# Last DeltaNet head and its block inverse: VectorE's panel residuals, tile sums and inverse levels in another order

## What is computed

```
proj = h @ w_in
qkv = silu(causal_depthwise_conv(proj[..., :DN_CONV_DIM], conv_w))
lower = where(strict, einsum("bhncd,bhnkd->bhnck", k_beta, k) * decay, 0)
sol = triangular_solve(lower + eye(CHUNK), rhs, lower=True)
u, w = sol[..., :DN_DV], sol[..., DN_DV:]
def step(state, xs):
    v_new = u_n - w_n @ state
    o = q_n @ state + a_n @ v_new
    state = state * exp(gl_n) + k_n.T @ v_new
o = rmsnorm(o, norm_w) * silu(z)
h = h + o @ w_out
hn = rmsnorm(h, norm_mlp[0]);  h = h + square(relu(hn @ mlp_w_up[0])) @ mlp_w_down[0]
```

## Time and profile before

| | |
|---|---|
| median of 3 runs | 1400.56 us (1398.73 to 1401.97) |
| profiled execution | 1400.85 us |
| its span | 1399.1 us |
| TensorE busy | 1358.9 us, 97% |
| VectorE busy | 793.7 us, 57% |
| ScalarE busy | 532.4 us, 38% |
| GpSimd busy | 250.5 us, 18% |
| mean granted clock of TensorE | 0.993 of full speed |

### The profile page before, as it was taken

The page is one execution under the profiler, slowest core; times in us unless marked ns, Lnnn a source line. Parts: engine busy times, 40 slices in busy tenths (PEclk is TensorE's granted clock), DMA queues, the critical chain, the costliest instruction groups (busy, mean ns, idle before and its releaser), DMA issues.

```text
span 1399.1 us, 18107 instructions
## 1 busy us (share of the span) xinstructions
PE 1358.9 (97%) x6594; PEld 1118.9 (80%) x6594; DVE 793.7 (57%) x1205; ACT 532.4 (38%) x901; POOL 250.5 (18%) x243
## 2 busy tenths in 40 slices
PE   7989999999899999999999999989999999999998
PEld 5778888888778888888888878668888888888877
DVE  5567787777674343343465876764433434335755
ACT  6545545443253141331334421654322323223344
POOL 3545555553031000000012110002010000000211
PEclk9999999999999999999999999999999999999998
DMA  6233332322232223222322353312232322332211
GB/s 177 66 86 86 79 79 62 85 70 71 90 106 91 90 98 113 90 90 93 104 76 89 103 123 70 82 43 94 91 101 94 107 90 90 100 104 98 89 62 60
DMA packets 168575, 125.67 MB, mean 90 GB/s; under 512 B 35873, under 2 KB 165186, under 8 KB 168514
## 3 DMA queue, kind: packets, MB, share of 16 engines
q1 hardware_dynamic: 167410, 123.01, 29.6%
q10 hardware_dynamic: 1104, 1.84, 0.5%
HBM read 116.96 MB, written 5.25 MB: 87 GB/s over the span
## 4 chain that ended last, share of the span: by engine, by line
PE 79%; DVE 11%; ACT 3%; issue 2%; DVEq 2%; DMA 1%; POOL 1%; POOLq 0%; SPq 0%; ACTq 0%
PE psum L148 22%; PE psum L150 22%; PE psum L149 22%; PE psum L898 2%; DVE wL L140 1%; PE psum L909 1%; ACT wH L132 1%; DVE bL L1408 1%; DVEq L1177 1%; DVE hT L1609 1%; DVE terms L1175 1%; DVE acc L1607 1%; PE psum L1928 1%; PE psum L912 1%; PE psum L1935 1%
## 5 line engine op out<-in xcount | busy, mean ns | idle before, releaser
L148 PE MATMUL psum<-aH,wH 128*128 128x512 f32 x896 | 360.4, 402 | 4.0 <-ACT taps L744 3.4
L150 PE MATMUL psum<-aL,wH 128*128 128x512 f32 x896 | 350.7, 391 | 0.0
L149 PE MATMUL psum<-aH,wL 128*128 128x512 f32 x896 | 349.8, 390 | 0.0
L140 DVE TENSOR_TENSOR wL<-wRaw,wH 128x2048 fp32r<-128x2048 f32 (+2 forms) x125 | 240.0, 1924 | 132.7 <-ACT wH L132 127.1
L148 PE MATMUL psum<-bH,wH 128*128 128x512 f32 x720 | 284.6, 395 | 2.3 <-DVE pleT L2054 1.6
L150 PE MATMUL psum<-bL,wH 128*128 128x512 f32 x720 | 280.9, 390 | 0.0
L132 ACT CAST wH<-wRaw 128x2048 fp32r<-128x2048 f32 (+2 forms) x109 | 197.2, 1814 | 219.9 <-PE psum L150 219.9
L149 PE MATMUL psum<-bH,wL 128*128 128x512 f32 x720 | 280.7, 390 | 0.0
L148 PEld LDWEIGHTS psum<-aH,wH 128*128 128x128 f32 x896 | 169.0, 189 | 37.6 <-ACT taps L744 3.9
L150 PEld LDWEIGHTS psum<-aL,wH 128*128 128x128 f32 x896 | 168.5, 188 | 36.1
L149 PEld LDWEIGHTS psum<-aH,wL 128*128 128x128 f32 x896 | 169.1, 189 | 32.0 <-issue 0.5
(11 more groups left out here) (295 smaller groups left out, 1503.4 us busy)
## 6 DMA issues: line engine op xcount, KB each, us to landing
wRaw<-in_mlp_w_up SPq DMA_DIRECT2D x64, 512.0 KB
wRaw<-in_mlp_w_down SPq DMA_DIRECT2D x64, 512.0 KB
wRaw<-in_dn_w_in SPq DMA_DIRECT2D x32, 512.0 KB
wRaw<-in_ple_w_gate SPq DMA_DIRECT2D x16, 512.0 KB
xScaled<-inv_blocks SPq DMA_DIRECT2D x16, 256.0 KB, 3.1
wRaw<-in_sw_w_in SPq DMA_DIRECT2D x16, 256.0 KB
wRaw<-in_sw_w_out SPq DMA_DIRECT2D x16, 256.0 KB
wRaw<-in_dn_w_out SPq DMA_DIRECT2D x8, 384.0 KB
```

Of the source, the lines that this page charges most:

```text
L140: last = [nc.vector.tensor_tensor(o, r, h_.bitcast(F32), ALU.subtract) for o, r, h_ in zip(*([v if half is None else v[:, half * v.shape[1 ...
L148: nc.tensor.matmul(o, wh, xh, start=first, stop=False)
L149: nc.tensor.matmul(o, wl, xh, start=False, stop=False)
L150: return nc.tensor.matmul(o, wh, xl, start=False, stop=last)
```

## The change

It moves instructions of VectorE, and one of ScalarE. In every step but the last: the second half of the residual of the panel in slot 1 goes from before `advance(1)` to behind `residual(2)`; `blocks_inverse(4)` goes before `residual(2)`; `blocks_inverse(8)` is split into its two halves with `solved(2)` between them. At the end of head 7's step the tile sum `out_early_dve(4)` and the next panel's residual go behind the last scan's `advance(0)`. In the last scan the residual of the last output panel comes in halves around `solved(3)` instead of after the scan, `tail(0)` comes before `out_early_dve(6)`, and ScalarE's cast of that panel comes before its `q_part(3)`. In `dn_last_dve` the residual of the MLP's first panel comes in halves behind tiles 1 and 3 instead of ahead of all tiles.

```diff
@@ dn_step_act
             if a is None:
-                for i in range(1, NT):
-                    q_part(i)
+                q_part(1)
+                q_part(2)
                 prep_hi(act, n, n % 2)
+                q_part(3)
                 tail(0)
                 tail(1)
@@ dn_step_dve
             if a is None:
                 solved(0)
                 advance(0)
+                out_early_dve(dve, 4)
+                prep_lo(dve, n - 1, (n - 1) % 2)
                 for i in range(1, NT):
                     residual(i)
+                    if i == 3:
+                        prep_lo(dve, n, n % 2, 0)
                     solved(i)
                     if i == 2:
                         out_early_dve(dve, 5)
+                    if i == 3:
+                        prep_lo(dve, n, n % 2, 1)
                     advance(i)
+                tail(0)
                 out_early_dve(dve, 6)
-                prep_lo(dve, n, n % 2)
-                tail(0)
                 tail(1)
...
-            def blocks_inverse(m):
+            def blocks_inverse(m, parts=(0, 1)):
...
-                for left, right, out_ in ((low, first, hf), (second.rearrange("p q c i -> p q i c"), hf, corner)):
+                steps = ((low, first, hf), (second.rearrange("p q c i -> p q i c"), hf, corner))
+                for left, right, out_ in (steps[i] for i in parts):
...
             residual(1)
             prep_lo(dve, n, 1, 0)
             solved(1)
-            prep_lo(dve, n, 1, 1)
             if p is not None:
                 g_next_dve(dve, p)
             silu_dve(dve, a, 2, a_, reused)
             advance(1)
             pairs_inverse()
             blocks_inverse(2)
+            blocks_inverse(4)
             residual(2)
-            blocks_inverse(4)
+            prep_lo(dve, n, 1, 1)
             if p is None:
                 out_early_dve(dve, 0)
-            solved(2)
             if b is None:
                 silu_dve(dve, p, 0, s, reused)
-            blocks_inverse(8)
+            blocks_inverse(8, (0,))
+            solved(2)
+            blocks_inverse(8, (1,))
             blocks_out()
             advance(2)
...
             grown(2)
-            if p is None:
-                out_early_dve(dve, 4)
-                prep_lo(dve, n + 2, 1)
             dve.drain()
@@ dn_last_dve
-            prep_lo(dve, N_MLP0, N_MLP0 % 2)
             for m in range(KT):
                 dve.wait_ge(tile_done, tiles_before(N_DNLAST) + m + 1)
                 nc.vector.tensor_tensor(hT[:, m, :], bank[2 + m % 4], hT[:, m, :], ALU.add).then_inc(res_ok, 1)
                 if m:
                     next_dve(dve, 0, m - 1)
+                if m in (1, 3):
+                    prep_lo(dve, N_MLP0, N_MLP0 % 2, m // 2)
```

## The result

The changed kernel takes 1404.64 us (median of 12 runs, 1402.43 to 1410.01); the kernel before, run beside it, 1398.46 us (median of 12 runs). The ratio is 1.0044, interval 1.0032 to 1.0056: slower by 0.44%, as forecast in kind, against 0.32% by my sum. The profiled execution of the changed kernel took 1403.45 us with a span of 1401.5 us. I therefore read from the traces where time went, stretch by stretch, and from the medians how much.

A forecast was written before the change was run, and what follows sets the result against it. The prediction took TensorE, busy 1358.9 of 1399.1 us, as the bound, so only its waits and lower-clock stretches count. Its parts, +6.2 + 1.7 - 0.1 - 3.4 = +4.4 us, gave 1405.0 us, range 1397.8 to 1408.0 us.

The forecast's parts named there:

- Part 1: Looped steps, heads 1 to 6: vNew moves behind a half of level 8, net 1.0 us a head, +6.2 us.
- the walk's wait: Looped steps: walk(3)'s wait of 0.30 us for the state goes, since the state is there in time.
- rival (3): Looped heads: three of six go each way in the order of multiplication and tap sum; +1.2 us, 1401.8 us, chance 0.18.
- Part 2: Head 0's step: the moved half residual makes TensorE wait, less old waits that go, plus one lower-clock stretch; +1.7 us.
- the 13 units: Head 0: TensorE's units 16 to 28, each three 128x512 products; from 73.7 they need 9.0 us.
- The wait at unit 16: Head 0: TensorE waits 3.5 to 4.9 us at the first unit needing the moved panel's residual.
- Part 3: Head 7's step: update(2) waits about 0.5 us, but the product behind waits for the DMA anyway; -0.1 us.
- Part 4, scan: Last scan: waits and a lower-clock stretch go, new waits at solve(1) and vNew(3) come; -3.8 us.
- The two waits that were to go: Last scan: TensorE's waits before 362.64 and before 381.95 go, -2.0 us and -2.1 us.
- the wait for rT: Last scan: a new TensorE wait of 1.3 us at solve(1), from work moved behind advance(0).
- rival (4): Head 0 and last scan: the new waits are each followed by the lower clock; +7.8 us, 1408.4 us, chance 0.07.
- Part 4, hand-over: Behind the last scan, up to the sixth aL: DVE is the bound and 0.4 us of the gain are lost.

The follow-up runs named there:

- experiment 1: Changed kernel with the last scan, ScalarE's order and the hand-over to the MLP as before, so only the heads' edits: 1405.27 us, ratio 1.0049.
- experiment 7: Changed kernel with the slot-1 residual's second half put back in head 0's step alone: 1403.45 us, ratio 1.0028.
- experiment 3: Kernel before with only the hand-over edit, the first MLP panel's residual in halves behind tiles 1 and 3: 1402.78 us, ratio 1.0016.
- experiment 2: Kernel before with only the last scan's edits: 1399.53 us, ratio 0.9987.
- experiment 5: Changed kernel, GpSimd's first tap sum in heads 1 to 6 waiting by semaphore for VectorE's level-8 multiplication: 1398.17 us, ratio 0.9993.
- experiment 6: Changed kernel, VectorE drained ahead of the level-8 multiplication in looped heads so GpSimd's tap sum is first: 1404.59 us, ratio 1.0048.
- experiment 4: Changed kernel with the slot-1 residual's second half back ahead of advance(1) in all steps: 1396.43 us, ratio 0.9978.
- 8: Kernel of experiment 4 with the hand-over as before and the last scan's 1536-column residual in halves behind advance(0) and advance(1): 1393.25 us, ratio 0.9954.

## Why the prediction was right, and where its sizes were off

The likeliest case held in its direction (slower, chance 0.50): the median, against the kernel run beside it, lies 6.2 us above, and the forecast was 4.4 us. The parts, by its own steps:

- **Part 1, +6.2 us forecast, +4.2 us in the trace.** The mechanism was right in each link: vNew behind a half of level 8, the multiplication of 1 us taking 2.05 us behind the tap sum, a wait of 1.34 us at update(2) (1.3 forecast), the walk's wait gone, net 1.0 us a head. Wrong was that one order would hold in all six. The sum put the two starts 0.01 us apart; they were 0.14 to 0.39 us apart in heads 1, 2, 3 and 5, and 0.02 us in heads 4 and 6, which go the other way. This is rival (3) in its mechanism, with four heads instead of three. The whole cost (5.7 us) and its opposite (-0.6 us) came when the order was forced.
- **The gap between two instructions.** I took from the pair in the earlier trace rows that a waiting GpSimd instruction gets in between the residual and the multiplication. It does where its record starts 0.14 us or more ahead, and in head 4 of experiment 1 with 0.04 us; it doesn't in the five cases with 0.02 or 0.03 us (heads 4 and 6 of the changed kernel and of experiment 7, head 6 of experiment 1). The Trainium skill ("SBUF — State Buffer", on the two separate sides) gives the whole instruction to whichever starts first; in head 4 the tap sum's record starts first (227.70 against 227.72) and it is the one that is held up. So at such distances the order of the records isn't the order in which the side was taken. Where it comes further ahead the record holds some waiting too (1.38 us in head 3 for 1.28 of work): there the residual is still running, and the record's start is read as the start of waiting. That reading fits the rows but no run tests it.
- **Part 2, +1.7 us forecast.** The residual's end was put between 72.3 and 73.7 and came at 73.45; the wait between 3.5 and 4.9 us and was 4.80. The mis-sized term is the lower clock behind it: from 73.51 the 13 units should have needed 9.0 us, to 82.5, but L898 starts at 85.32 without waiting, so the clock took 2.8 us and not 1.7; the step is 2.7 us longer, inside the bounds. Experiment 7 adds what the sum left out: with the residual back the step is still 1.5 us longer than in the trace before, since there the lower clock came ahead of the wait for the DMA, which hid it, and here behind. That stretch of the trace before was thus no cost of 1.7 us, as the prediction has it: without it (experiment 3) the step takes 40.0 us against 40.4. From these two traces 1.3 us of the 2.7 would be the residual's. How sure that is, the step's lengths say: 40.4, 43.2 and 40.0 us with the code before (before, experiments 2 and 3), 43.2, 42.5, 41.7 and 42.9 with the changed one (changed, 1, 5 and 6), 41.7, 41.9 and 41.3 with the residual back (4, 7 and 8). The wait at unit 16 is there in each of the four, 4.8 to 5.6 us long, but what it costs in the step isn't separated from the clock.
- **Part 3, -0.1 us forecast.** -0.2 us in the trace.
- **Part 4, scan: -3.8 us forecast, -4.3 us.** The two waits that were to go went; the wait for rT was 1.07 us (1.3 forecast). That the sum came close here is luck. Its term of 1.7 us for the lower clock behind the first wait was read from one execution; the same wait in the same code wasn't followed by it in experiments 1 and 3, and against those the edits gain 2.7 us. vNew(3) cost 0.21 us, not 0.7: the half ran in 1.13 us up to the next start while TensorE still had its own work. No lower clock followed the wait for rT, so rival (4) did not hold there.
- **Part 4, hand-over: +0.4 us forecast, +1.7 us in the trace,** and by experiment 3 a ratio of 1.0016. This is the term that was furthest off for its size. "DVE's work from the first tile sum to that point is unchanged" counted instructions and not their time: the halves moved from a place where GpSimd is idle to one where it adds squares, and took 1.63 and 2.28 us for 2 x 1.22. It is the same turn-taking that Part 1 was built on; I applied it there and forgot it here.

In the trace the parts sum up to +4.1 us where +4.4 was forecast: the heads were milder by 2.0 us and the scan better by 0.5, against 1.3 more in the hand-over and 1.0 more in head 0. Against a last scan without the lower clock (35.3 us) the same parts sum up to +5.6 us, nearer to the 6.2 us of the medians. That the sum came close to the trace is in part luck.

Open: what the last scan's edits gain on average, since it hangs on how often the lower clock follows the wait that they remove, and what head 0 costs. The last 1000 us, which no kernel changes, took 998 to 1001 us in nine of the ten traces and 1004.6 in experiment 2's.

## What to carry to other kernels

When a VectorE instruction with two large SBUF operands is moved, look at what GpSimd does at the new place before anything else: an instruction of 1.0 or 1.2 us becomes one of 2.1 or 2.3 us there, and it isn't in the count of work. Where such a race lies ahead of something that TensorE waits for, don't leave its outcome to a hundredth of a microsecond: make one side clearly early (experiment 4) or order it with a semaphore (experiment 5), and let the engine that nobody waits for be the second. And try the parts of a reordering apart: by the traces, at the sixth aL, the moved residual costs 8.0 us (402.41 against 394.37 in experiment 4) and the hand-over 1.7 us of a change whose other edits gain 5.8 us (1.5 of them the lower clock that fell in the last scan of the trace before). And take no stretch at the lower clock for a fixed cost that an edit will remove until a second trace of the same code shows it too.

## What the runs showed of the hardware that was not expected

- **A tie that other code decides.** In the changed kernel heads 4 and 6 went one way and 1, 2, 3, 5 the other, and in experiment 7 it was the same heads, while experiment 1, with the same code in those heads, had head 4 on the slow side (a lead of 0.04 us instead of 0.02). So which way a head goes doesn't carry over to a program that differs elsewhere. Whether it is the same in every execution of one program isn't shown: each was traced once.
- **The lower clock doesn't follow from the wait alone.** Before, a wait of 1.82 us at 76.23 was followed by the lower level (1.2 GHz). In experiment 2, whose instructions up to there are the same, the wait at 76.08 was again 1.82 us and wasn't followed by it; the clock fell at the wait for the DMA behind it (2.68 us):

```profile
76.00:82.00 6.00, 3.71 (x15) 2.74 (x15) 2.11 (x4) 2.45 (x3) 3.99 (x3) 0.99 0.32 67
80.00:90.00 10.00, 7.53 (x32) 6.78 (x32) 1.84 (x3) 0.63 (x1) 0.23 (x1) 0.66 0.60 159
```

  The wait of 2.13 us at 398.18 left the clock at its upper level in the changed kernel, and one of 2.12 us at the same product in experiment 6 was followed by this:

```profile
400.00:404.00 4.00, 4.00 (x11) 3.15 (x11) 4.00 (x7) 2.97 (x5) 2.05 (x2) 0.57 0.74 237
```

  And the wait of 1.96 us in the last scan was followed by it before and not in experiments 1 and 3 (1.97 us each).

- **The same step, three lengths.** The step of head 0 has the same instructions before and in experiments 2 and 3, and took 40.4, 43.2 and 40.0 us. In experiment 2 the lower clock came with the wait for the DMA (mean 0.66 over 80 to 90 us) and not ahead of it, where it is hidden; in experiment 3 that wait was 2.62 us and the clock didn't fall in the step (1.00 over 76 to 90 us). The Trainium skill ("TensorE: Matmul & The Clock Gate", on what is actually happening) calls the lower clock the state that idleness restores. These rows agree in that each of the stretches shown begins in a wait or behind one. That equal waits are followed by it or not makes a difference of some 3 us from one execution to another in this step alone, as large as the effects that were sought here.
